# Attention of a two-layer mixing trunk: heads in pairs, with the lane inversion packed into the middle of it

## What is computed

```python
# A, latent attention (4 heads, 96-wide q and k, 64-wide v); context rows see context only
p = softmax(einsum('bqhd,bkhd->bhqk', q, k) * scale); out = rms_norm(p @ v, gout)
# B, neighbourhood attention (4 heads of 64): window scores + bias + mask, joined with context scores
s = concatenate([s_win + bias, s_ctx]); out = rms_norm(softmax(s) @ v, gout)
# C, gated DeltaNet in chunks: a unit lower triangular matrix of each chunk has to be inverted
lmat = where(strict, (kb @ kc^T) * decay, 0)
sol  = triangular_solve(lmat, rhs, lower=True, unit_diagonal=True)
```

## Time and profile before

| | us |
|---|---|
| median of 3 runs (2400.2 to 2402.36) | 2401.79 |
| the profiled execution's own time | 2400.78 |
| its span, first to last instruction | 2399.0 |
| PE busy | 2194.1 (91%) |
| DVE busy | 1095.3 (46%) |
| ACT busy | 867.1 (36%) |
| POOL busy | 195.9 (8%) |
| mean granted TensorE clock | 0.944 |

### The profile page before, as it was taken

How to read it: one execution, slowest core, us unless ns; L and a number is a source line. 1 busy time by engine, 2 the same in 40 slices (tenths; PEclk the granted TensorE clock), 3 DMA queues, 4 the chain that set the end, 5 groups by cost and what they waited for, 6 DMA issues and landing times.

```text
span 2399.0 us, 30801 instructions
## 1 busy us (share of the span) xinstructions
PE 2194.1 (91%) x12861; PEld 1819.9 (76%) x12861; DVE 1095.3 (46%) x1606; ACT 867.1 (36%) x1392; POOL 195.9 (8%) x196
## 2 busy tenths in 40 slices
PE   6889999899977997899999899999989987878997
PEld 4667878687755886688888688888768856767997
DVE  4223233566365356633333533333475366366555
ACT  3222223354354524422223432222343445334443
POOL 0000000100001342200000100000010002421000
PEclk8999999899989998999999899999978988988999
DMA  8454442423223324332432532432342321333662
GB/s 270 128 154 114 123 130 73 142 72 109 53 89 106 127 86 140 106 95 73 122 95 73 140 98 68 124 100 66 107 125 64 100 53 53 106 89 107 176 180 84
DMA packets 403322, 259.02 MB, mean 108 GB/s; under 512 B 21850, under 2 KB 401904, under 8 KB 403184
## 3 DMA queue, kind: packets, MB, share of 16 engines
q1 hardware_dynamic: 403184, 257.06, 37.0%
HBM read 255.97 MB, written 1.05 MB: 107 GB/s over the span
## 4 chain that ended last, share of the span: by engine, by line
PE 82%; DVE 9%; ACT 4%; issue 2%; SPq 1%; DMA 1%; POOL 1%; POOLq 0%; DVEq 0%; ACTq 0%
PE bank L788 22%; PE bank L790 21%; PE bank L789 21%; PE bank L711 2%; PE bank L1038 2%; PE bank L1061 1%; PE bank L1141 1%; PE bank L1155 1%; PE bank L1123 1%; PE bank L693 1%; PE bank L1050 1%; DVE wl L1843 1%; DVE uT L1907 1%; ACT arena L1701 1%; ACT mlaw L1612 1%
## 5 line engine op out<-in xcount | busy, mean ns | idle before, releaser
L788 PE MATMUL bank<-uh,wh 128*128 128x512 f32 (+1 forms) x1536 | 563.7, 367 | 34.3 <-DVE ul L1913 15.0
L789 PE MATMUL bank<-ul,wh 128*128 128x512 f32 (+1 forms) x1536 | 559.3, 364 | 0.0
L790 PE MATMUL bank<-uh,wl 128*128 128x512 f32 (+1 forms) x1536 | 559.1, 364 | 0.0
L1843 DVE TENSOR_TENSOR wl<-ring,wh 128x2048 fp32r<-128x2048 f32 (+1 forms) x157 | 317.1, 2020 | 187.4 <-ACT wh L1365 186.5
L1365 ACT ACTIVATE wh<-ring 128x2048 fp32r<-128x2048 f32 (+1 forms) x160 | 270.9, 1693 | 320.5 <-PE bank L790 305.2
L788 PEld LDWEIGHTS bank<-uh,wh 128*128 128x128 f32 x1536 | 294.8, 192 | 88.9 <-issue 34.3
L790 PEld LDWEIGHTS bank<-uh,wl 128*128 128x128 f32 x1536 | 294.2, 192 | 45.3
L789 PEld LDWEIGHTS bank<-ul,wh 128*128 128x128 f32 x1536 | 294.9, 192 | 43.5
L788 PE MATMUL bank<-hh,wh 128*128 128x512 f32 (+1 forms) x704 | 255.5, 363 | 1.4 <-DVE wl L1843 1.4
L789 PE MATMUL bank<-hl,wh 128*128 128x512 f32 (+1 forms) x704 | 255.2, 362 | 0.0
L790 PE MATMUL bank<-hh,wl 128*128 128x512 f32 (+1 forms) x704 | 255.2, 362 | 0.0
(11 more groups left out here) (298 smaller groups left out, 2935.1 us busy)
## 6 DMA issues: line engine op xcount, KB each, us to landing
ring<-in_ffn_w_dram SPq DMA_DIRECT2D x176, 512.0 KB, 5.2
ring<-in_w_mod_dram SPq DMA_DIRECT2D x136, 512.0 KB, 4.6
ring<-in_ffn_w_dram SPq DMA_DIRECT2D x64, 384.0 KB, 3.6
ring<-in_ffn_w_dram SPq DMA_DIRECT2D x64, 320.0 KB, 4.2
ring<-in_w_in_dram SPq DMA_DIRECT2D x40, 512.0 KB, 4.7
ring<-in_w_out_dram SPq DMA_DIRECT2D x16, 512.0 KB, 4.6
arena<-in_w_mod_dram SPq DMA_DIRECT2D x8, 512.0 KB, 9.2
ring<-in_w_in_dram SPq DMA_DIRECT2D x4, 544.0 KB, 5.1
```

The source lines that it names most:

```text
L788: pe.matmul(bank, w_hi, x_hi, start=first, stop=False)
L789: pe.matmul(bank, w_hi, x_lo, start=False, stop=False)
L790: return pe.matmul(bank, w_lo, x_hi, start=False, stop=last)
L1843: TT(low[:, b, 0:floats], at, high[:, b, 0:floats].bitcast(F32), ALU.subtract).then_inc(wl_ready, 1)
```

## The change

Attention goes by pairs of units (heads h and h + 1 of one tile): 16 pairs in layer 0, 8 in layer 1.

- PE: four banks of scores; both scores of a pair, then both biases. `weigh(p)` now has v as weights (64 columns) and the turned probabilities moving (128 columns), one head in each half of bank 6, so that the output is feature-major; two more matmuls spread the reciprocal of the row sums over it. Turns use banks 4 and 5. Attention waits at its start for mla_v_copied.
- DVE: LANE_STEPS = (4, 8) steps per pair from pair 2 on, so lanes take pairs 2 to 9 in layer 0 and 2 to 5 in layer 1. `lanes_end` is split: `lanes_flip` at the last of these pairs, `lanes_turn` a pair later. `scale(p)` is a copy out of bank 6 and a product of 128x128.
- ACT: exponentials and copies by pairs. `place(0)` moves into attention, as `place_inverse` one pair and `place_solved` two pairs after the turn. The squares of the attention output move from attention into slot 1 (`att_squares`), the root into slot 2 (`att_roots`, now 128x256).
- GpSimd copies the diagonal blocks, 8 copies per tile as soon as the tile is ready, so in `chunks`. They go to lane_b, and lane_a and lane_b change roles in `lanes_begin` and the steps.
- levels: the turning of the attention output (PE) and its copies (ACT) go; PE sums the squares in slot 2 and spreads the inverse roots in slot 3; DVE takes the reciprocal (`att_inverses`) at the head of slot 2 and scales four blocks of 128x512 (layer 1: 128x256) behind slot 3.
- Modulation pieces: the same 11 and 5, spread evenly over the pairs, in bank 7.

```diff
+        LANE_STEPS = (4, 8)
+        def lane_pairs(l):
+            return 2 + -(-31 // LANE_STEPS[l])
+        def lane_steps(l, p):
+            each = LANE_STEPS[l]
+            return range(each * (p - 2), min(each * (p - 1), 31)) if 2 <= p < lane_pairs(l) else ()
...
+                def weigh(p):
+                    mx, t, h = units[2 * p]
                     v = (mlav, natv)[mx]
...
+                    pe.wait_ge(sem("att_turned_copied"), u0 + 2 * p + 2)
+                    if u0 + p:
+                        pe.wait_ge(sem("att_out"), u0 // 2 + p)
                     for b in range(keys(t)):
...
+                        for r in range(2):
+                            last = pe.matmul(ps[6][64 * r:64 * r + 64, 0:P], v[:, b, (h + r) * 64:(h + r + 1) * 64],
+                                             probT[:, r, b * P:(b + 1) * P], start=b == 0, stop=b == keys(t) - 1)
                     last.then_inc(sem("att_weighed"), 1)
...
+                    pe.wait_ge(sem("att_inverse"), u0 // 2 + p + 1)
+                    for r in range(2):
+                        c = 12 + (2 * p + r) % 4
+                        last = pe.matmul(ps[6][64 * r:64 * r + 64, P:2 * P], small[:, c:c + 1].to_broadcast([P, 64]),
+                                         ident, start=True, stop=True)
+                    last.then_inc(sem("att_spread"), 1)
+                for p in range(pairs + 2):
+                    if p and att_mod(l, p - 1) is not None:
+                        mod_turn(att_mod(l, p - 1), ps[7])
+                    if p < pairs:
+                        scores(2 * p)
+                        scores(2 * p + 1)
+                        biases(2 * p)
+                        biases(2 * p + 1)
+                    if p >= 2:
+                        weigh(p - 2)
+                    if 1 <= p <= pairs:
+                        turn(2 * p - 2)
+                        turn(2 * p - 1)
+                    if att_mod(l, p) is not None:
+                        mod_product(att_mod(l, p), ps[7], att_mod(l, p))
...
+                elif slot == 2:
+                    pe.wait_ge(sem("kb_copied"), 4 * (l + 1))
+                    att_sums(l)
+                elif slot == 3:
+                    att_spread(l)
...
+                    if p == lane_pairs(l) + 1:
+                        act.wait_ge(sem("lanes_turned"), l + 1)
+                        act.wait_ge(sem("ut_zero"), l + 1)
+                        place_inverse(l, 0)
+                    if p == lane_pairs(l) + 2:
+                        place_solved(l, 0)
...
+                act.wait_ge(sem("att_sums"), l + 1)
+                at = quadrants(halves(l, True))
+                A(att_root[at, :, :], ps[0][at, 0:2 * P].rearrange("p (m n) -> p m n", m=2), ACT.Sqrt,
+                  bias=epsc[at, 0:1], scale=1.0 / 256).then_inc(sem("att_std"), 1)
...
+                    if slot == 1:
+                        att_squares(l)
+                elif slot == 2:
+                    att_roots(l)
...
-                act.wait_ge(sem("lanes_turned"), l + 1)
-                act.wait_ge(sem("ut_zero"), l + 1)
-                place(0)
-                att_roots(l)
...
+                def scale(p):
+                    mx, t, h = units[2 * p]
+                    dve.wait_ge(sem("att_spread"), u0 // 2 + p + 1)
+                    link(V.tensor_copy(att_scale, ps[6][:, P:2 * P]))
+                    TT(att_o[:, 2 * mx + h // 2, t * P:(t + 1) * P], ps[6][:, 0:P], att_scale, ALU.mult
+                       ).then_inc(sem("att_out"), 1)
+                for p in range(pairs + 2):
+                    if p == pairs // 2 - 2:
+                        mask_bias(l)
+                    steps = lane_steps(l, p)
+                    for i in range(max(2, len(steps))):
+                        if i < len(steps):
+                            lane_first(steps[i])
+                        if i < 2 and p < pairs:
+                            top(2 * p + i)
+                        if i < len(steps):
+                            lane_second(steps[i])
+                    if p == 1:
                         lanes_begin(l)
...
+                    if 1 <= p <= pairs:
+                        inverse_sums(p - 1)
+                    if p >= 2:
+                        scale(p - 2)
+                    if p == lane_pairs(l) - 1:
+                        lanes_flip(l)
+                    if p == lane_pairs(l):
+                        lanes_turn(l)
+            def att_inverses(l):
+                dve.wait_ge(sem("att_std"), l + 1)
+                at = quadrants(halves(l, True))
+                V.reciprocal(att_root[at, :, :], att_root[at, :, :]).then_inc(sem("att_norm_inverse"), 1)
 
             def att_norm(l):
...
+                dve.wait_ge(sem("att_norm_spread"), l + 1)
+                t0 = HALF * halves(l, True)[0]
+                for b in range(4):
+                    last = STT(uT[:, b, t0:T], att_o[:, b, t0:T], prm[:, l, 189 + b:190 + b], ps[b // 2][:, t0:T],
+                               ALU.mult, ALU.mult)
+                last.then_inc(sem("att_scaled"), 1)
...
+                        if (t, s) == (1, 0):
+                            att_inverses(l)
...
-                        if t == 0 and s == 0:
+                        if (t, s) == (1, 1):
                             att_norm(l)
...
-                pool.wait_ge(sem("mla_v"), 2 * (l + 1))
-                G.memset(Tms[0][:, :, :], 0.0).then_inc(sem("tm_zero"), 1)
+                for t in range(NT):
+                    pool.wait_ge(sem("lt_ready"), (l * NT + t) * 2 + 2)
+                    for q in range(4):
+                        o = slice(32 * q, 32 * q + 32)
+                        at = lane_b[o, :, :].rearrange("p i (d t h) -> p d t h i", d=2, t=NT)
+                        for d in range(2):
+                            last = G.tensor_copy(at[:, d, t], LT[o, d, t, :].rearrange("p (h n) -> p h n", h=NH)[:, :, o])
+                    last.then_inc(sem("diag_copied"), 1)
                 pool.wait_ge(sem("att_scores"), ATT_BEFORE[l] + len(att_units(l)) // 2)
                 G.memset(UT[:, :, :, :], 0.0).then_inc(sem("ut_zero"), 1)
-                pool.wait_ge(sem("att_turned"), ATT_BEFORE[l + 1])
-                G.memset(Tms[1][:, :, :], 0.0).then_inc(sem("tm_zero"), 1)
-                pool.wait_ge(sem("att_weighed"), ATT_BEFORE[l + 1])
+                pool.wait_ge(sem("att_turned"), ATT_BEFORE[l] + late(l))
+                G.memset(Tms[0][:, :, :], 0.0).then_inc(sem("tm_zero"), 1)
+                pool.wait_ge(sem("att_scores"), ATT_BEFORE[l + 1])```

DVE in layer 0, one stretch of attention: before, two units, each with one lane step (L2162, L2169), a maximum (L2190), and reciprocal and scale (L2196, L2198).

```order
L2169 TENSOR_TENSOR arena<-arena,mlaw 128x20x12 [waits lane_multiplied]
L2196 RECIPROCAL small<-small 128x1 [waits att_exp]
L2198 TENSOR_SCALAR uT<-bank4,small 128x64 [waits att_weighed,dve_link]
L2162 TENSOR_TENSOR mlaw<-mlaw,arena 128x247 [waits lane_updated]
L2190 TENSOR_REDUCE small<-bank1 128x1 [waits att_scores]
L2169 TENSOR_TENSOR arena<-arena,mlaw 128x19x13 [waits lane_multiplied]
L2196 RECIPROCAL small<-small 128x1 [waits att_exp]
L2198 TENSOR_SCALAR uT<-bank5,small 128x64 [waits att_weighed,dve_link]
```

More of the change, by code:

```diff
@@ L1063, in weigh @@
                     last.then_inc(sem("att_weighed"), 1)
-                for u in range(len(units) + 2):
-                    if u < len(units):
-                        scores(u)
-                    if 1 <= u <= len(units):
-                        turn(u - 1)
-                    if u >= 2:
-                        weigh(u - 2)
-                    if u and att_mod(l, u - 1) is not None:
-                        mod_turn(att_mod(l, u - 1), ps[6])
-                    if att_mod(l, u) is not None:
-                        mod_product(att_mod(l, u), ps[6], att_mod(l, u))
@@ L1658, in attention @@
-                squares(N - 1)
+                        act.wait_ge(sem("att_weighed"), (u0 + u) // 2)
+                    A(probT[:, u % 2, 0:n], ps[4 + u % 2][:, 0:n], ACT.Copy).then_inc(sem("att_turned_copied"), 1)
+                for p in range(pairs + 1):
+                    if p < pairs:
+                        exp(2 * p)
+                    if p and att_mod(l, p - 1) is not None:
+                        mod_column_out(att_mod(l, p - 1), ps[7])
+                    if p < pairs:
+                        exp(2 * p + 1)
+                    if p:
+                        copy(2 * p - 2)
+                        copy(2 * p - 1)
+                    if att_mod(l, p) is not None:
+                        mod_row_out(att_mod(l, p), ps[7])
+                    if p == lane_pairs(l) + 1:
[4 more added lines that the diff above has]
+                        place_solved(l, 0)
```

234 lines of the change are left out of this document (92 added, 142 removed).

## The result

| | before | changed |
|---|---|---|
| median of four runs, us | 2400.99 (2397.08 to 2402.36) | 2373.85 (2371.51 to 2374.76) |
| ratio, 95% interval | | 0.9888 [0.9871, 0.9905] |
| span of the profiled execution | 2399.0 | 2371.6 |
| layer 0: first score to first level product | 104.7 | 84.5 |
| layer 0: first level product to the last second product | 56.3 | 60.8 |

What follows compares the result with a forecast made beforehand. It took attention and its levels to be bound by unfed TensorE at head and tail, and by instruction pace between. Terms -20.1, -14.1, +11.2, +1.0 and -0.7 sum to -22.7 against 2400.8: 2378 us, range 2365 to 2394.

Steps and rivals of the forecast that it cites:

- Part 1: Layer 0 attention, following the slower of DVE and PE through the pairs: levels start at 759.6 for 779.75, -20.1 us.
- 42.7 + 4.6: Layer 0 attention, DVE's time: 42.7 us for pairs 2 to 9, 4.6 for pair 10 with the transposes.
- 22.0 + 4.1: Layer 0 attention, PE's end: pairs 12 to 15 at 5.5 us each, 22.0, then 4.1 to drain the last two.
- the 6.5: Sign against the forecast: pairs over 6.5 us where PE leads would prove it wrong.
- The bare prices: Attention: instruction prices without mode-change drains, such as two heads' scores at 2.1 us, or 1.1 if side by side.
- the rival that drains: Some 7 pairs of layer 0: weight loads wait 0.41 us at two mode changes a pair, +5.7, 2384; chance 0.06.
- up to 1.0 it stays free: Head of layer 0 attention: GpSimd's diagonal copies, taken at 0.4 us each, stay hidden up to 1.0 each.
- Part 2: Layer 1 attention, 8 pairs, DVE leading from start to end: levels start at 2009.8 for 2023.9, -14.1 us.
- the rival's level: Cold clock: PE fed about 55% in layer 1, at 1.2 GHz; 2387 to 2396, chance 0.20.
- Part 3: Levels, slot 2: DVE's reciprocal waits for ACT's root behind eight placings; +5.6 us a layer, +11.2.
- Part 4: Clock: first level product faster, -1.8 in layer 0, -0.9 in layer 1; +1 a layer after slot 2's idle; together -0.7.
- the +1.0: Levels: PE's wait for the scalings at slot 4, +0.5 us a layer.

Runs made afterwards that it cites:

- only_pool_copies: The kernel before with only the diagonal copies moved from ScalarE to GpSimd, the two lane buffers exchanged for it: 2387.44 us, ratio 0.9933.
- mod_late: The changed kernel with the turn of a modulation column behind the pair's scores and biases on TensorE, not ahead of them: 2364.29 us, ratio 0.9846.
- root_first: The changed kernel with the root of the attention sums ahead of the eight placings in ScalarE's slot 2 of the levels: 2360.45 us, ratio 0.9827.
- place_late: The changed kernel with tile 0's eight placings moved out of attention, back to the start of the levels on ScalarE: 2387.41 us, ratio 0.9933.
- pool_twice: The changed kernel with GpSimd's eight copies of the last tile done twice, the second set into a buffer nothing reads: 2376.81 us, ratio 0.9895.

## Why the prediction was right, by its steps

**Part 1, layer 0 attention: right in the sum, -20.1 for -20.15 (759.60), by two errors that cancel.** That they cancel is luck. VectorE's part was shorter. From the end of lanes_begin to the end of the transposes it took 45.0 (681.13 to 726.1), where 42.7 + 4.6 = 47.3 were predicted, and it began 2.1 earlier, since the four tops, in one run from 675.79 to 677.51, come ahead of the modulation turn. Most of the 2.3 is one term, the flip: it was taken at 3.7, by the earlier trace rows, and takes 2.0:

```profile
719.66 0.74 DVE L2209 TENSOR_SCALAR arena<-arena,cst 128x1024 f32<-128x1024 f32 x1
720.44 1.28 DVE L2210 SCALAR_TENSOR_TENSOR arena<-arena,cst 128x1024 f32<-128x1024 f32 x1
```

These are the operations of L2176 and L2177, on the same shapes, which took 1.59 and 2.16 in the kernel before. There two GpSimd products ran beside them, which the rows of VectorE alone do not show:

```profile
767.47 2.93 POOL L2583 TENSOR_TENSOR arena<-arena,cst 128x512 f32<-128x512 f32 x2 [0.90 <-PE bank L1061]
```

In only_pool_copies the flip still stands beside them and takes the same 1.59 and 2.16.

PE's part was longer by what VectorE's was shorter. Pair 12 starts at 730.32, 3.2 ahead of the sum's 733.5, and from there to the levels it takes 29.3 where 22.0 + 4.1 were added up. The pairs 12, 13 and 14 start at 730.32, 733.83, 740.66, and the next at 748.78, so 18.5 for three where 5.5 each was taken; two of them are over the 6.5 that the prediction named as a sign of being wrong.

```profile
734.76 2.58 ACT L1656 ACTIVATE arena<-mlaw 32x256 f32<-32x256 f32 x4
734.89 1.13 PE L1062 MATMUL bank<-uT,cst 128*128 128x256 f32 x4
...
735.95 0.66 PE L1083 MATMUL bank<-arena 128*64 128x128 f32 x8
736.44 0.39 PE L1089 MATMUL bank<-cst,small 128*64 128x128 f32 x4
736.75 1.09 PE L1071 MATMUL bank<-cst,arena 128*128 128x128 f32 x8
...
737.37 0.69 ACT L1675 ACTIVATE arena<-bank,small 128x512 f32<-128x512 f32 x1
737.78 1.07 PE L729 MATMUL bank<-ring,scT 128*32 128x256 f32 x16
...
739.67 0.40 ACT L1383 ACTIVATE mod_row<-bank 128x256 f32<-128x256 f32 x1
740.12 0.61 PE L711 MATMUL bank<-cst,mod_row 128*128 128x2 f32 x4 [1.27 <-ACT mod_row L1383]
```

This is pair 13's iteration, layer 0. A placing of 2.58 holds back the exponential to 737.37, that the copies, these the row at 739.67, and PE stands at the turn. Three things that the sum had at nothing lie behind pair 12, and the runs price them. The turn ahead of the scores costs 2.0: with it behind them the part is 25.7 (mod_late), for 27.7 (root_first) with the clock at 1.00 in both. The fall of the clock costs 1.6. The placings ("falls into pairs 11 and 12 and is done") cost 0.7: without them pair 14 starts 6.1 behind pair 13 and not 6.8 (place_late). The diff showed both moves, that of the turn and that of the placings; of the first nothing was priced, of the second only whether it was done in time.

The bare prices held. Two scores of different heads do run side by side: four matmuls of 64 rows and 512 columns take 1.13, the cheaper of the two values given. Weighing takes 1.09 busy for 512 keys, spreading 0.39. In the rows above weighing follows the bias, and the turns the spreading, without a gap between PE's own instructions, so the rival that drains cost 0.41 twice a pair is out: the Trainium skill, TensorEngine Tiling (Array Packing), Key Properties, names a drain at each change of mode, and here it does not show beyond 0.1 us on the path.

**GpSimd's copies: price right, cover wrong.** A copy takes 0.40 in the median of 32 (0.4 was taken). But "up to 1.0 it stays free ... 32 copies of 1.0 end at 680" counted all 32 from tile 0, though the last eight can't start before tile 3 is ready, at 675.06. At 1.0 they would end at 683.1. pool_twice shows the cover: 0.7 us in layer 0.

**Part 2, layer 1 attention: -15.9 for -14.1.** 59.8 from first score to levels, 61.6 predicted. The flip is 2.0 for 3.7 here too, nearly the whole difference. The order was as described, place last: it ends at 1990.43 and the level product starts at 1990.48. The clock did fall for a while, but not to the rival's level: granted 0.91 over the stage (1930.7 to 1990.5), for 0.60 in the rival's row.

**Part 3, the stall: right in place, chain and size.** Predicted: root done 9.7 and reciprocal 11.5 after slot 2's first product starts. Measured: 9.5 and 11.3 (780.60 and 782.39, from 771.13). Slot 3's product follows slot 2's by 12.45 and 12.6, for 6.2 and 5.8 before: +6.2 and +6.8, where +5.6 was given for each layer. In slot 4 PE waits 1.6 for the scalings, where 0.5 was put in the sum. The levels as a whole took +4.5 and +6.0, so +10.5, where part 3, part 4 and the +1.0 make 11.5. root_first takes 12.8 away.

**Part 4, clock: right in kind.** The first level product takes 2.05 in both layers, for 3.66 and 3.78, as said. Slot 0 as a whole is 1.6 and 2.4 shorter (1.8 and 0.9 were given), slot 3 behind the stall 1.5 longer in both layers (1.0 was given); place_late shows that a cold start costs the whole of slot 0, 2.6, and not the one product only. One place no term had: slot 5 of layer 0. It takes 7.9 in the kernel before and in only_pool_copies, which start it at a granted clock of 0.50, and 6.65 in every kernel with the change. It is one reason why the levels, with part 3 larger than given, still came out 1.0 under the sum; the other is slot 4, which is 0.3 shorter and 0.2 longer in the two layers where the sum had 0.5 longer each.

**What remains.** The sum's 2378.1 against 2373.44, the profiled execution's own time, is 4.7: 1.8 in layer 1's attention, 1.0 in the levels, 1.8 in the stretch between that nothing touches.

## What to carry to other kernels

When an edit puts a wait at the head of an in-order queue, look for the instruction that it waits for and ask what stands ahead of that on its own queue: moving that one instruction gave 13 us, moving the waiting one half as much. A step that is moved without being changed, as the modulation turn was, needs its producer's place checked on the other engine as well as its own length. Dense work of one engine was best spread thinly over the units of the other: up to pair 12, 3, 4 and 5 steps a pair cost 50, 55 and 61 us for the same lanes, the clock's part included. And before a duration is carried from one stretch to another, look at what the neighbour engine did beside it: the flip was priced at 3.7 from rows with GpSimd at work, and takes 2.0 without.

## What the runs showed of the hardware

Twelve small copies on VectorE (64 partitions by 2 elements, L2301) take 1.04 in all in layer 1, ahead of GpSimd's products. In layer 0 they meet GpSimd at work:

```profile
760.25 4.04 DVE L2301 COPY std<-gates 64x2 f32<-64x2 f32 x12
```

```profile
760.84 2.53 POOL L2638 TENSOR_TENSOR arena<-arena,cst 128x512 f32<-128x512 f32 x2 [7.27 <-PE bank L1183]
763.31 0.94 POOL L2628 MEMSET arena<- 128x1024 f32 x1
```

That is 3.0 more; the copies end at 764.29, as GpSimd's memset does (764.25). The flip of the lanes shows the same on two larger instructions: beside GpSimd's products 1.59 and 2.16, alone 0.74 and 1.28. The Trainium skill, SBUF — State Buffer, Terms, describes a port pair that the two engines lock for a whole instruction; the rows agree, by their times. Here it cost nothing that the stage shows: the subtraction behind them comes 1.8 after the first second product (762.6 to 764.41), and in place_late, where the copies were long over, it does too (763.38 to 765.22).

The granted clock also fell in stretches where PE was busy: from 740 to 745 it was 0.72 with PE busy for 4.88 of 5.00, behind ten us at 1.00 with PE busy for 8.85. In root_first and pool_twice, with the same instructions there, it stayed at 1.00. No run tells what set this off. And the longest of GpSimd's 32 copies took 1.38 and 1.39 in the two layers for a median of 0.40; the cause stays open.
